# Twenty-four products of the state-space stage, on VectorE instead of GpSimd

## What is computed

```python
y = y + d_skip.astype(f32)[:, None] * xs
y = y.reshape(bsz, L, D_INNER) * jax.nn.silu(z.astype(f32))
yg = y.reshape(bsz, L, SSM_GROUPS, D_INNER // SSM_GROUPS)
yg = yg * lax.rsqrt(jnp.mean(yg * yg, axis=-1, keepdims=True) + NORM_EPS)
y = yg.reshape(bsz, L, D_INNER) * gate_norm.astype(f32)
out = y.astype(h.dtype) @ w_out
```

## Time and profile before

| what | value |
|---|---|
| timed runs | 2466.86, 2468.47, 2468.60 us, median 2468.47 |
| profiled execution | 2464.5 us, its span 2462.9 us |
| TensorE busy | 2387.5 us (97%) |
| VectorE busy | 1205.2 us (49%) |
| ScalarE busy | 844.2 us (34%) |
| GpSimd busy | 326.7 us (13%) |
| mean granted clock of TensorE | 0.989 of full speed |

### The profile page before, as it was taken

One profiled execution on the slowest core, in us unless ns is written; L12 is line 12 of the kernel. 1 busy time (PEld: TensorE's weight loads), 2 busy tenths in 40 slices (PEclk: granted clock), 3 DMA queues, 4 the chain that ended last, 5 costly groups with the idle time before them and its releaser, 6 DMA issues.

```text
span 2462.9 us, 45809 instructions
## 1 busy us (share of the span) xinstructions
PE 2387.5 (97%) x18206; PEld 2338.2 (95%) x18206; DVE 1205.2 (49%) x1477; ACT 844.2 (34%) x1334; POOL 326.7 (13%) x277
## 2 busy tenths in 40 slices
PE   8999999899999999999999999999999899999997
PEld 8999999889888899999999999999988799999997
DVE  6344332778899944443433434343336564434323
ACT  4222222456667622222222322222226532222212
POOL 0000011323333221000011100000222240000021
PEclk9999999999999999999999999999999989999999
DMA  3222222335555422222222222222241122222222
GB/s 132 85 85 77 86 88 91 117 116 185 174 176 175 138 84 79 85 77 85 80 90 85 77 85 80 82 85 85 86 120 35 35 69 85 78 84 85 84 87 81
DMA packets 66193, 234.88 MB, mean 95 GB/s; under 512 B 7888, under 2 KB 8016, under 8 KB 65968
## 3 DMA queue, kind: packets, MB, share of 16 engines
q1 hardware_dynamic: 52560, 187.72, 22.9%
q0 software_dynamic: 8320, 31.52, 4.0%
q10 hardware_dynamic: 5248, 14.76, 1.9%
HBM read 221.31 MB, written 14.64 MB: 96 GB/s over the span
## 4 chain that ended last, share of the span: by engine, by line
PE 86%; DVE 5%; issue 5%; ACT 1%; POOL 1%; DMA 1%; ACTq 0%; DVEq 0%; POOLq 0%
PE psum L410 74%; PE psum L428 6%; DVE cacc L1450 1%; PE psum L705 1%; POOL probs L2009 1%; DVE wlo L1331 1%; PE psum L838 1%; PE psum L482 1%; PE psum L596 1%; PE psum L601 1%; DVE grs L1686 0%; PE psum L631 0%; DMA E<-decay_rows 0%; ACT whi L906 0%; PE psum L623 0%
## 5 line engine op out<-in xcount | busy, mean ns | idle before, releaser
L1331 DVE TENSOR_TENSOR wlo<-wraw,whi 128x1024 fp32r<-128x1024 f32 x342 | 436.5, 1276 | 981.9 <-ACT whi L906 981.8
L906 ACT ACTIVATE whi<-wraw 128x1024 fp32r<-128x1024 f32 x349 | 369.4, 1059 | 934.5 <-PE psum L410 903.7
L410 PE MATMUL psum<-xhi,whi 128*128 128x288 f32 x3008 | 647.7, 297 | 11.0 <-POOL wlo L2025 6.9
L410 PE MATMUL psum<-xlo,whi 128*128 128x288 f32 x3008 | 645.6, 296 | 0.0
L410 PE MATMUL psum<-xhi,wlo 128*128 128x288 f32 x3008 | 645.2, 296 | 0.0
L410 PEld LDWEIGHTS psum<-xhi,whi 128*128 128x128 f32 x3008 | 486.6, 189 | 13.0 <-issue 12.4
L410 PEld LDWEIGHTS psum<-xhi,wlo 128*128 128x128 f32 x3008 | 486.3, 189 | 0.0
L410 PEld LDWEIGHTS psum<-xlo,whi 128*128 128x128 f32 x3008 | 486.2, 189 | 0.0
L410 PE MATMUL psum<-hhi,wlo 128*128 128x288 f32 x1408 | 302.6, 296 | 0.0
L410 PE MATMUL psum<-hhi,whi 128*128 128x288 f32 x1408 | 302.6, 296 | 0.0
L410 PE MATMUL psum<-hlo,whi 128*128 128x288 f32 x1408 | 302.6, 296 | 0.0
(11 more groups left out here) (285 smaller groups left out, 2519.7 us busy)
## 6 DMA issues: line engine op xcount, KB each, us to landing
wraw<-w SPq DMA_DIRECT2D x349, 512.0 KB, 3.4
seg<-decay_rows ACTq DMA_DIRECT2D x16, 576.0 KB, 4.3
h0s<-ssm_state POOLq DMA_DIRECT2D x16, 512.0 KB, 5.3
h0T<-ssm_state_t POOLq DMA_DIRECT2D x16, 512.0 KB, 3.8
ssm_s<-h0s POOLq DMA_DIRECT2D x16, 512.0 KB, 3.5
E<-decay_rows ACTq DMA_DIRECT2D x32, 144.0 KB, 4.0
x<-x_in SPq DMA_DIRECT2D x8, 288.0 KB, 6.7
y<-ybuf SPq DMA_DIRECT2D x8, 288.0 KB, 2.4
```

The source lines that it names most:

```text
L410: last = pe.matmul(acc[:, 2 * pair + half, 0:HALF], wt[s][:, k * P:(k + 1) * P], m[:, k0 + k, half * HALF:(half + 1) * HALF], start=start ...
L906: act.activation(whi[n % 2][:], wraw[n % 2][:], ACT.Copy).then_inc(weights_hi, 1)
L1331: dve.tensor_tensor(wlo[n % 2][:], wraw[n % 2][:], whi[n % 2][:].bitcast(F32), ALU.subtract).then_inc(weights_lo, 1)
```

## The change

`group_add` and `normalised` move from GpSimd's list to VectorE's, with the same operands, waits and semaphores: 12 sums of squares and 12 products, each 128x576 in float32. Nothing else that is computed moves. Where they come on VectorE:

- `group_add(p)` comes in a later body behind the first `split_lo`, ahead of `conv_in`; that of tile 14 in `last`, ahead of `z_out`; that of tile 15 behind the last `gated`.
- `normalised` comes, in bodies 8 and 12, right behind that `group_add`, so that `grs` is read before the next group overwrites it; in the other bodies behind `sample_final`, ahead of `low_part` and `conv_out`; the tiles 10 and 11 in `last`, between `z_gate` and `low_part(6)`.

So bodies 2, 3 and 4 get one sum, bodies 5, 9 and 13 one product, bodies 6, 7, 8, 10, 11, 12 and 14 one of each, and `last` one sum and two products, with one more sum behind it. VectorE's bodies are unrolled to the same extent as GpSimd's were; GpSimd's go back into loops.

```diff
+                def group_add(p, added_before):
+
+                    dve.wait_ge(ysq, added_before + 1)
+                    dve.tensor_tensor(gsum[:], gsum[:], thz[:], ALU.add).then_inc(gsum_step, 1)
+
+                def normalised(p, g):
+
+                    dve.wait_ge(grstd, 2 * g + 2)
+                    dve.tensor_tensor(yall[:, p, :], yall[:, p, :], grs[:], ALU.mult).then_inc(yn_ready, 1)
+
-                def body(p, g, first=False, stats=None, early=()):
+                def body(p, g, first=False, stats=None, early=(), norm=None, added=None):
...
                         split_lo(n + 2, 2 * p)
+                    if added is not None:
+                        group_add(*added)
+                    if norm is not None and stats is not None:
+                        normalised(*norm)
                     dve.wait_ge(units_done, n + 2 * p + 2)
                     conv_in(j, j + 2 * GROUPS, 0)
...
                     sample_final(p)
+                    if norm is not None and stats is None:
+                        normalised(*norm)
                     for k in early:
                         low_part(k)
...
                     split_lo(n + 2, 2 * p)
+                    group_add(14, 10)
                     z_out(p, n + 2 * p + 2)
...
                     z_gate(p)
+                    normalised(10, 2)
+                    normalised(11, 2)
                     low_part(6)
                     low_part(7)
...
-                with dve.Fori(1, 4) as p:
-                    body(p, 0)
-                for g in range(1, GROUPS - 1):
-                    body(g * 4, g, stats=g - 1)
-                    with dve.Fori(1, 4) as q:
-                        body(g * 4 + q, g)
-                body(12, GROUPS - 1, stats=GROUPS - 2)
-                body(13, GROUPS - 1, early=(0, 1))
-                body(14, GROUPS - 1, early=(2, 3))
-                last(NX - 1, GROUPS - 1)
-                opened(NX - 1)
-                gated(NX - 1)
+                body(1, 0)
+                with dve.Fori(2, 4) as p:
+                    body(p, 0, added=(p - 1, p - 2))
+                body(4, 1, stats=0, added=(3, 2))
+                body(5, 1, norm=(0, 0))
+                with dve.Fori(6, 8) as p:
+                    body(p, 1, norm=(p - 5, 0), added=(p - 1, p - 3))
+                body(8, 2, stats=1, norm=(3, 0), added=(7, 5))
...
+                body(12, 3, stats=2, norm=(7, 1), added=(11, 8))
+                body(13, 3, early=(0, 1), norm=(8, 2))
+                body(14, 3, early=(2, 3), norm=(9, 2), added=(13, 9))
+                last(15, 3)
+                opened(15)
+                gated(15)
+                group_add(15, 11)
...
-                    pool.wait_ge(ysq, added_before + 1)
-                    pool.tensor_tensor(gsum[:], gsum[:], thz[:], ALU.add).then_inc(gsum_step, 1)
...
-                    pool.wait_ge(grstd, 2 * g + 2)
-                    pool.tensor_tensor(yall[:, p, :], yall[:, p, :], grs[:], ALU.mult).then_inc(yn_ready, 1)
...
-                body(15, 3, more=False, norm=(10, 2), added=(14, 10))
-                group_add(15, 11)
+                body(NX - 1, more=False)
```

More of the change, by code:

```diff
@@ L1661, in heads @@
                 body(0, 0, first=True)
-                with dve.Fori(1, 4) as p:
-                    body(p, 0)
-                for g in range(1, GROUPS - 1):
-                    body(g * 4, g, stats=g - 1)
-                    with dve.Fori(1, 4) as q:
-                        body(g * 4 + q, g)
-                body(12, GROUPS - 1, stats=GROUPS - 2)
-                body(13, GROUPS - 1, early=(0, 1))
-                body(14, GROUPS - 1, early=(2, 3))
-                last(NX - 1, GROUPS - 1)
-                opened(NX - 1)
-                gated(NX - 1)
+                body(1, 0)
[6 more added lines that the diff above has]
+                body(8, 2, stats=1, norm=(3, 0), added=(7, 5))
+                body(9, 2, norm=(4, 1))
+                with dve.Fori(10, 12) as p:
+                    body(p, 2, norm=(p - 5, 1), added=(p - 1, p - 4))
+                body(12, 3, stats=2, norm=(7, 1), added=(11, 8))
[5 more added lines that the diff above has]
+                group_add(15, 11)
             def group_var(g, *banks):
@@ L1918, in heads, with body @@
                 m = TILE["xz"]
-                def group_add(p, added_before):
-                    pool.wait_ge(ysq, added_before + 1)
-                    pool.tensor_tensor(gsum[:], gsum[:], thz[:], ALU.add).then_inc(gsum_step, 1)
-                def normalised(p, g):
-                    pool.wait_ge(grstd, 2 * g + 2)
-                    pool.tensor_tensor(yall[:, p, :], yall[:, p, :], grs[:], ALU.mult).then_inc(yn_ready, 1)
[L1930 to L1936, removed]
+                def body(p, more=True):
                     if more:
@@ L1959, in heads @@
                 sequence_b(0, first=True)
-                body(0, 0)
-                body(1, 0)
-                with pool.Fori(2, 4) as p:
-                    body(p, 0, added=(p - 1, p - 2))
-                sequence_b(1)
-                body(4, 1, added=(3, 2))
-                body(5, 1, norm=(0, 0))
-                with pool.Fori(6, 8) as p:
-                    body(p, 1, norm=(p - 5, 0), added=(p - 1, p - 3))
-                sequence_b(2)
-                body(8, 2, norm=(3, 0), added=(7, 5))
-                body(9, 2, norm=(4, 1))
-                with pool.Fori(10, 12) as p:
-                    body(p, 2, norm=(p - 5, 1), added=(p - 1, p - 4))
-                sequence_b(3)
-                body(12, 3, norm=(7, 1), added=(11, 8))
-                body(13, 3, norm=(8, 2))
-                body(14, 3, norm=(9, 2), added=(13, 9))
-                body(15, 3, more=False, norm=(10, 2), added=(14, 10))
-                group_add(15, 11)
+                body(0)
+                with pool.Fori(1, 4) as p:
+                    body(p)
+                with pool.Fori(1, GROUPS - 1) as g:
+                    sequence_b(g)
+                    with pool.Fori(0, 4) as q:
+                        body(g * 4 + q)
+                sequence_b(3)
+                with pool.Fori(12, NX - 1) as p:
+                    body(p)
+                body(NX - 1, more=False)
                 pool.wait_ge(conv_saved, 2 * NXBC)
```

## The result

| comparison | after, median (runs) | before, median (runs) | ratio, 95% interval |
|---|---|---|---|
| first | 2453.24 us (6) | 2467.76 us (6) | 0.9950 [0.9929, 0.9972] |
| second | 2455.87 us (9) | 2465.27 us (31) | 0.9966 [0.9952, 0.9981] |
| third | 2454.80 us (12) | 2465.69 us (18) | 0.9959 [0.9944, 0.9974] |

The kernel after is faster, by 9 to 15 us; the forecast was 4.8 and a time of 2463.7. Its profiled execution took 2454.64 us with a span of 2453.1. VectorE does 24 instructions more and is busy 1198.3 us, not 1205.2; GpSimd falls from 326.7 to 290.9 us.

A forecast was written before the change was run, and what follows sets the result against it. TensorE (97% busy) bounds early bodies, VectorE, stretched by GpSimd's products, nearly as much the later ones. Terms 7.1 - 0.5 + 1.6 - 3.4 = 4.8 us off the median 2468.47 gave 2463.7 us; range 2457 to 2469.

The forecast's parts named there:

- L596 waits: TensorE's state products waiting for VectorE's `xdd`: all waits but body 0's 1.4 us go, gaining 7.1 us.
- L428, bodies 13 and 14: Projection product waiting for `z_out`: 0.7 us lost after body 13, 0.2 gained at body 14's end, sum -0.5 us.
- clock in bodies 14 and 15: Slow clock after body 15's 2.24 us wait goes with that wait, gaining 1.6 us.
- tail: After the last body: longer waits cost 1.8 us and a clock fall 1.6, together -3.4 us.
- stage: State-space stage with its tail: the terms sum to a gain of 4.8 us.
- L705's wait of 1.62 us grows by 1.8: In the tail, VectorE is 1.8 us late at `opened(15)` and one chain passes this on to L705's wait.
- The fall of the clock: Behind the tail's 2.8 us wait TensorE's clock falls, costing 1.6 us, between bounds of 0 and 1.6.
- L428 behind body 13: Sign of being right: TensorE's projection product waits about 0.9 us after body 13.
- The rule of the Trainium skill: VectorE with two SBUF inputs and GpSimd reading SBUF exclude each other, first starter winning; `xdd` loses up to 0.7 us, bodies 8, 12.
- The wait moves: Rival, chance 0.20: waits move from L596 to L428 if each moved product costs 1.0 us; gain 3.1 us, 2465.4.
- Slower: Rival, chance 0.08: something before GpSimd's products stretches L1547, so `xdd` stays late; about 9.5 us lost, 2478.
- The clock holds: Rival, chance 0.36: TensorE's clock does not fall in the tail; gain 6.4 us, 2462.1.

The follow-up runs named there:

- after_b: The changed kernel run again, unaltered, for a further trace; 2454.80 us (12 runs), stage 320.4 us.
- tiny: The changed kernel with its 24 moved products cut to 8 of 576 columns on VectorE; 2455.55 us, ratio to the kernel before 0.9965.
- sum_only: Against the changed kernel, the 12 products by the group's root stay on GpSimd, only the sums move; 2459.49 us, ratio to the kernel before 0.9978.
- norm_only: Against the changed kernel, the 12 sums of squares stay on GpSimd, only the products move; 2455.92 us, ratio to the kernel before 0.9967.
- shadow: The changed kernel plus 18 same-form GpSimd products on constants, never read, in bodies 2 to 13; 2464.23 us, ratio to the kernel before 1.0000.
- before_c: The kernel before, unaltered, run for a third trace; stage 330.7 us, medians of that kernel 2465.3 to 2467.8 us.
- after_c: The changed kernel, unaltered, run for a further trace; stage 322.0 us, medians of that kernel 2453.2 to 2455.9 us.
- pad10: The changed kernel with ten extra 128x288 TensorE products behind the state-space stage; 2462.09 us (12 runs), ratio to the kernel before 0.9976.

## Why the prediction was wrong

Its mechanism was right; the sizes of two terms in the stage were not, and the time that it started from was high. Each term against the means of three traces before and four after:

| term | predicted | measured | from |
|---|---|---|---|
| L596 waits | +7.1 | +7.7 | 7.1, 8.0, 8.0 before; 0 after |
| L428, bodies 13 and 14 | -0.5 | -0.5 | 0.8 before; 1.15, 2.06, 1.09, 1.09 after |
| clock in bodies 14 and 15 | +1.6 | +2.9 | from body 0 to 15: 303.4 less 293.4 is 10.05, less the two rows above; half of the slow stretches (3.4, 6.8, 6.8 us) is 2.8 |
| tail | -3.4 | -2.1 | 26.4 before; 28.9, 28.8, 27.3, 28.9 after |
| stage | 4.8 | 8.0 | 329.8 less 321.8 |

- **Two sizes failed, the tail first.** The step "L705's wait of 1.62 us grows by 1.8" failed: VectorE was to be 1.8 us late at `opened(15)` and to hand all of it on to L705. The waits there are 0.2 to 0.3 and 1.94: 0.5 to 0.65 us more than the 1.62 of before, and the tail of after_b, where the clock holds, is 0.9 us longer, not 1.8. The rows of the recorded trace of after and, behind the dots, of before show what became of it:

```profile
844.86 0.68 DVE L1568 TENSOR_TENSOR sqsum<-sqsum,psum 128x512 f32<-128x512 f32 x1
849.31 1.21 PE L715 MATMUL psum<-gsum,cst 128*128 128x288 f32 x4
858.94 2.76 DVE L1718 TENSOR_TENSOR yall<-yall,grs 128x576 f32<-128x576 f32 x4
...
854.19 1.21 PE L715 MATMUL psum<-gsum,cst 128*128 128x288 f32 x4
862.83 2.77 DVE L1693 TENSOR_TENSOR yall<-yall,grs 128x576 f32<-128x576 f32 x4
```

`opened(15)` (L1568) begins 1.3 us behind TensorE's last output product, not 1.8 (0.05 before). The statistics (L715) come 5.8 us behind the tail's first L705 in both traces, with no wait: up to there TensorE does not feel the delay. The four products behind them start 9.6 us after L715 (8.6 before). So 1.0 us reaches L705. The fall of the clock came in three traces of four and was rightly priced: 1.7 us each time.
- **The clock term was read from one trace.** The slow stretch of body 15 is 3.4 us long there and 6.8 us in the two others, at half clock. Nothing in the one trace said so; a second would have.
- **L596 went altogether, as predicted,** body 0's wait stays, and bodies 6, 7, 10 and 11 take 19.1 us. What the prediction did not ask is whether half of the change would do: in bodies 7, 8, 11 and 12 only both together outlast the slack.
- **L428 behind body 13:** predicted about 0.9, measured 0.84.
- **The rule of the Trainium skill** (SBUF — State Buffer, "Who interferes with whom"), by which `Bm` would still cost up to 0.7 us in bodies 8 and 12, found nothing to act on in after: `Bm` ends 0.3 us before `xdd` starts and begins as `gated`'s last sum ends. That is luck of the timing: in tiny, body 12, `Bm` begins 0.58 us after that sum (L1578) starts, and the sum takes 2.26 us, not 0.76 (beside the same overlap in bodies 4 and 8 it takes its 0.76). That VectorE is kept out to the end of GpSimd's instruction the traces bear out: in before, sum_only and norm_only every stretched `xdd` ends 0.55 to 0.57 us behind GpSimd's last product. That whichever starts first keeps the other out, as the prediction says, does not hold throughout: in body 7 `xdd` begins 0.10 us before GpSimd's product, in shadow L1582 0.44 us before `Bm`, in sum_only's body 14 L1578 0.63 us before a product (2.70 us for its 0.76), and VectorE was held each time, while GpSimd's instruction took its usual 1.05 to 1.44 us. The reverse is there once: GpSimd's last sum in before, at 852.09 us, begins 0.16 us behind a `low_part` and takes 1.95 us, not 1.4. What decides which of the two waits is not shown.
- **The rivals.** "The wait moves" needed 1.0 us a product; it takes 0.75, and bodies 1 to 13 are as long with the products as without (tiny). "Slower" is refuted by L1547's 0.69 us in after and by shadow. "The clock holds" is after_b, one trace of four.
- **The rest of the time.** The forecast of 2463.7 is 10.5 us above the first comparison's median: 3.2 is the stage, and it started from 2468.47, the median of three runs, where the 31 runs of before in the second comparison have 2465.27. Means of the three comparisons differ by 12.3, 8.9 and 10.4 us, 1 to 4 more than the stage. Behind the stage alone, executions of one kernel differ by up to 9 us. The range's low end, 2457, is about where 8.0 us below 2465 lies: no room was left for the scatter of six runs on top. Whether some of these 1 to 4 us belongs to the change stays open.

## What to carry to other kernels

Where one form of instruction has one duration alone and several times it elsewhere, look for what the neighbour engine does at that moment, and compare the excess with the slack: here company that stretched `xdd` cost nothing until the sum of it outlasted the slack, and then taking away either part paid. An instruction that is moved onto a busy engine did best in that engine's own waits here (behind `z_out`, for the tanh: the stage takes 318.9 and 318.6 us, 321.8 without). And before a term is read from one trace, ask how it varies: two more traces of the kernel before would have shown 1.7 of the 3.2 us by which the stage was under-priced.

## What was not expected of the hardware

TensorE has, in some executions, stretches in which it takes 771 matmuls per 100 us and not 752, at a granted clock of 1.00 in both. Windows of before and before_c, in the feed-forward:

```profile
1500.00:1600.00 100.00, 100.00 (x752) 100.00 (x751) 39.34 (x46) 27.92 (x32) 0.00 (x0) 1.00 0.26 84
```

```profile
1500.00:1600.00 100.00, 100.00 (x771) 100.00 (x770) 41.84 (x49) 27.93 (x32) 0.00 (x0) 1.00 0.26 84
```

In before_c this lasts from behind 1412 to between 1680 and 1700 us and saves about 7 us; after_c has it from before 100 to between 280 and 300 us; none of the other twelve traces has it in the hundreds looked at (100 to 400, 1000 to 1300, 1500 to 1800, 2100 to 2400 us). It may be a source of the lowest runs (2449.8 of before, 2445.9 of pad10); of those runs there are no traces, so this is not shown, and what sets it is open.
